# The remainder of nearly every weight tile is made by VectorE instead of GpSimd

## The reference, cut to what matters

```python
def second_block(x, ...):
    for i in range(2):
        h = rms_norm_2(x, attn_norm[i])
        proj = h @ w_in[i]                                  # differential attention, then gated linear
        mix = attention_i(proj)
        cross = memory_cross_attention(mem_q, mem, ...)
        x = x + concat([mix, cross]) @ w_out[i]
        h = rms_norm_2(x, ffn_norm[i])
        x = x + conv_ffn(h, w_up[i], conv_w[i], conv_b[i], w_down[i])

def conv_ffn(h, w_up, conv_w, conv_b, w_down):
    u = h @ w_up                                            # 1024 -> 2 * 2816
    a, g = split(causal_conv3(u, conv_w) + conv_b)
    return (silu(g) * a) @ w_down                           # 2816 -> 1024
```

## Time and profile before

| what | value |
|---|---|
| median of 3 runs | 1799.42 us (1798.91 to 1802.1) |
| profiled execution | 1797.66 us |
| its span in the trace | 1795.9 us |
| mean granted TensorE clock | 0.988 |
| TensorE busy | 1735.1 us, 97% |
| VectorE busy | 945.7 us, 53% |
| GpSimd busy | 746.8 us, 42% |

### The profile page before, as it was taken

How to read it: one execution, slowest core, us unless ns; L and a number is a source line. 1 busy time by engine, 2 the same in 40 slices (tenths; PEclk the granted TensorE clock), 3 DMA queues, 4 the chain that set the end, 5 groups by cost and what they waited for, 6 DMA issues and landing times.

```text
span 1795.9 us, 28022 instructions
## 1 busy us (share of the span) xinstructions
PE 1735.1 (97%) x11634; PEld 1403.9 (78%) x11634; DVE 945.7 (53%) x1610; ACT 477.8 (27%) x1039; POOL 746.8 (42%) x372
## 2 busy tenths in 40 slices
PE   8999989999899999899999999999999999999999
PEld 7678768887667777777888888877876788888887
DVE  6676245666655376746655551234434466665311
ACT  3111123445232354423222220123121332222100
POOL 3333135200544132237555554553233665555542
PEclk9999999999899999999999999999999999999999
DMA  5222120000234122113223322221112233323332
GB/s 194 83 82 88 44 87 3 3 3 3 89 109 139 46 97 74 59 59 106 96 94 96 103 95 94 95 91 59 59 58 71 74 94 102 97 94 95 104 95 71
DMA packets 43644, 143.95 MB, mean 80 GB/s; under 512 B 5191, under 2 KB 7128, under 8 KB 43390
## 3 DMA queue, kind: packets, MB, share of 16 engines
q1 hardware_dynamic: 43518, 142.15, 24.8%
HBM read 139.50 MB, written 4.08 MB: 80 GB/s over the span
## 4 chain that ended last, share of the span: by engine, by line
PE 66%; DVE 3%; ACT 2%; issue 1%; POOL 0%; DMA 0%; DVEq 0%; SPq 0%; ACTq 0%
PE all_p_bank L214 20%; PE all_p_bank L216 19%; PE all_p_bank L215 19%; PE all_p_bank L2553 1%; PE all_p_bank L2582 1%; PE all_p_bank L2340 1%; PE all_p_bank L2316 1%; PE all_p_bank L2570 0%; PE all_p_bank L2067 0%; PE all_p_bank L3050 0%; PE all_p_bank L3032 0%; PE all_p_bank L3045 0%; PE all_p_bank L2327 0%; POOL b_wlo L195 0%; PE all_p_bank L2516 0%
## 5 line engine op out<-in xcount | busy, mean ns | idle before, releaser
L195 POOL TENSOR_TENSOR b_wlo<-b_raw,b_whi 128x1024 fp32r<-128x1024 f32 x235 | 576.2, 2455 | 748.2 <-DVE b_whi L181 745.6
L214 PE MATMUL all_p_bank<-b_hi,b_whi 128*128 128x512 f32 x1232 | 498.7, 405 | 7.7 <-issue 6.1
L216 PE MATMUL all_p_bank<-b_hi,b_wlo 128*128 128x512 f32 x1232 | 482.8, 392 | 0.0
L215 PE MATMUL all_p_bank<-b_lo,b_whi 128*128 128x512 f32 x1232 | 482.7, 392 | 0.0
L181 DVE CAST b_whi<-b_raw 128x1024 fp32r<-128x1024 f32 x238 | 184.7, 782 | 424.1 <-PE all_p_bank L216 410.3
L214 PEld LDWEIGHTS all_p_bank<-b_hi,b_whi 128*128 128x128 f32 x1232 | 233.0, 189 | 72.4 <-issue 26.1
L216 PEld LDWEIGHTS all_p_bank<-b_hi,b_wlo 128*128 128x128 f32 x1232 | 232.9, 189 | 49.9
L215 PEld LDWEIGHTS all_p_bank<-b_lo,b_whi 128*128 128x128 f32 x1232 | 233.0, 189 | 49.5 <-issue 4.1
L214 PE MATMUL all_p_bank<-f_mhi,b_whi 128*128 128x512 f32 x352 | 136.9, 389 | 0.0
L215 PE MATMUL all_p_bank<-f_mlo,b_whi 128*128 128x512 f32 x352 | 136.9, 389 | 0.0
L216 PE MATMUL all_p_bank<-f_mhi,b_wlo 128*128 128x512 f32 x352 | 136.9, 389 | 0.0
(11 more groups left out here) (459 smaller groups left out, 2566.4 us busy)
## 6 DMA issues: line engine op xcount, KB each, us to landing
b_raw<-in_w_up SPq DMA_DIRECT2D x88, 512.0 KB, 3.5
b_raw<-in_w_down SPq DMA_DIRECT2D x44, 512.0 KB, 3.5
b_raw<-in_w_in SPq DMA_DIRECT2D x32, 512.0 KB, 3.5
b_raw<-in_w_out SPq DMA_DIRECT2D x24, 512.0 KB, 3.6
b_raw<-in_w_gla SPq DMA_DIRECT2D x22, 512.0 KB, 3.5
b_raw<-in_w_diff SPq DMA_DIRECT2D x20, 512.0 KB, 3.5
b_raw<-in_w_mem SPq DMA_DIRECT2D x8, 512.0 KB, 3.6
all_x<-in_x SPq DMA_DIRECT2D x8, 256.0 KB, 5.6
```

The source lines that it names most:

```text
L195: self.nc.gpsimd.tensor_tensor(self.lo[:, n % SLOTS, :], self.raw[:, n % RAWS, :], self.hi[:, n % SLOTS, :].bitcast(F32), ALU.subtract).th ...
L214: nc.tensor.matmul(acc, lhsT=left[0], rhs=right[0], start=first, stop=False)
L215: nc.tensor.matmul(acc, lhsT=left[0], rhs=right[1], start=False, stop=False)
L216: return nc.tensor.matmul(acc, lhsT=left[1], rhs=right[0], start=False, stop=last)
```

## The change

A list of ranges of tiles is added to the ring. For a tile in a range, VectorE makes the remainder right behind its cast, and GpSimd skips it. The one range goes from the second program's fifth tile to the last tile of all. At the border each engine waits once for the other (`s_lo`), so that the remainders are counted in order: VectorE's first remainder waits for GpSimd's last. Nothing else is written differently: the plan, the loads and TensorE's list stay.

```diff
@@ class Ring
+        self.ranges = []
@@ def round(self, dve, upto)
             self.nc.vector.tensor_copy(self.hi[:, n % SLOTS, :], self.raw[:, n % RAWS, :]).then_inc(self.s_hi, 1)
             self.rounded = n + 1
+            if self.whole(n):
+                if not self.whole(n - 1):
+                    dve.wait_ge(self.s_lo, n)
+                self.low(dve, n)
+
+    def whole(self, n):
+
+        return any(a <= n < b for a, b in self.ranges)
 
     def split(self, dve, n):
 
         self.round(dve, n)
+        self.low(dve, n)
+
+    def low(self, dve, n):
+
         dve.wait_ge(self.s_hi, n + 1)
         self.nc.vector.tensor_tensor(self.lo[:, n % SLOTS, :], self.raw[:, n % RAWS, :],
                                      self.hi[:, n % SLOTS, :].bitcast(F32), ALU.subtract).then_inc(self.s_lo, 1)
@@ def rest(self, pool, upto)
         for n in range(self.rested, min(upto + 1, len(self.tiles), self.limit)):
+            self.rested = n + 1
+            if self.whole(n):
+                continue
+            if self.whole(n - 1):
+                pool.wait_ge(self.s_lo, n)
             pool.wait_ge(self.s_hi, n + 1)
             self.nc.gpsimd.tensor_tensor(...)
-            self.rested = n + 1
@@ def upper_layers
+    c.ring.ranges = [(base + 4, len(c.ring.tiles))]
     run(nc, u.ring, base, plan + plan3, TwoLayers(low, high), Sides(*side, *side3), begin, store)
```

## The result

The changed kernel takes 1813.26 us (median of 4 runs, 1810.76 to 1814.18), the one before 1799.78 us on the same chip. The ratio is 1.0070, 95% interval 1.0057 to 1.0083. So the change costs 13.5 us by the medians and 12.6 by the ratio, where I had forecast 0.4 us less, that is no difference. The profiled execution has a span of 1812.4 us against 1795.9; it is the longest of the four and the one before the shortest of its kernel, so the 16.5 us between them are more than the change costs.

A forecast was written before the change was run, and what follows sets the result against it. TensorE, busy 97% of the span, was taken as the bound. Five places summed to -0.45 us, other waits and feed-forward blocks to nothing: 1799.42 - 0.45 = 1799.0 us, forecast's own range 1796.5 to 1801.5, 8 in 10 1794 to 1803.5.

The forecast's parts named there:

- Price of a moved remainder: Each remainder moved to VectorE adds 1.25 us to its list where nothing hides it; bounds 1.23 and 2.455.
- What is given back: VectorE operations stretched during GpSimd's subtractions fall back to short values, such as 2.82 to 0.68 us at line 2616.
- The five places: Five TensorE waits in the attention stages, 9.1 us together, that the change touches most; net sum -0.45 us.
- at 650: TensorE's wait of 1.09 us at 650.72: one cast's remainder adds 1.25, line 2656 gives back 0.39; net +0.86.
- the chain of 747 and 759: TensorE's waits of 2.99 and 3.01 us, one chain on VectorE and ScalarE from 740.10 on; net -1.4 us.
- 1238: TensorE's wait of 1.26 us at 1238.39: two casts add 0.7, line 2366 gives back 1.85; net -1.16.
- 1376: TensorE's wait of 0.76 us at 1376.69: remainder stands before a bank's emptying, nothing given back; net +1.25.
- The other waits of the attention stages: Remaining attention waits and the two norms ahead of the feed-forward blocks: taken as 0, bounded by say 2 us.
- Feed-forward blocks cost nothing: In the feed-forward blocks each pair has 3.4 us to spare, falling to 2.2, so TensorE sees nothing.
- Faster by the clock: Rival: shorter waits spare two stretches at 1.2 GHz behind 747 and 759; -3.9 us, 1795.5 us; chance 0.20.
- Nothing is given back: Rival: long VectorE rows have another cause, or the lock only changes hands; +6.8, 1806.2 us; chance 0.12.
- Taps late by 21 us: Rival: taps too late by 0.5 in each of 42 feed-forward pairs; +21 us, 1820 us; chance 0.03.

The follow-up runs named there:

- e2: Against the kernel before, VectorE makes the remainders of layer two's 40 attention tiles alone; 1802.92 us, ratio 1.0018.
- e12: Against the kernel before, VectorE makes the remainders of layer three's 30 attention tiles except four, which stay with GpSimd; 1797.98 us, ratio 0.9997.
- e5: The changed kernel's 202 remainders on VectorE, each made one to three steps later in its list; 1801.82 us, ratio 1.0021 to the kernel before.
- e1: Against the kernel before, VectorE makes the remainders of the two feed-forward blocks' 132 tiles alone; 1802.02 us, ratio 1.0010.
- e10: Against the kernel before, VectorE makes six attention tiles' remainders, one pair's only behind a side step; 1796.05 us, ratio 0.9971.

## Why the prediction was wrong, step by step

- **Price of a moved remainder, 1.25 us of the list: right**, 0.69 and 1.23 in the rows at 632. But only 163 of 205 took 1.22 or 1.23 us. The other 42 took 2.19 or 2.20, each beside a GpSimd operation:

```profile
867.63 0.69 DVE L182 CAST b_whi<-b_raw 128x1024 fp32r<-128x1024 f32 x1 [0.46 <-PE all_p_bank L233]
867.91 1.56 POOL L756 TENSOR_TENSOR f_mlo<-f_m,f_mhi 128x512 fp32r<-128x512 f32 x1 [9.32 <-ACT f_mhi L740]
868.36 2.20 DVE L201 TENSOR_TENSOR b_wlo<-b_raw,b_whi 128x1024 fp32r<-128x1024 f32 x1
```

The mean, 1424 ns, missed the 1.22 to 1.3 that I had named. These rows are what the sentence cited from the Trainium skill ("SBUF — State Buffer", "SBUF: two separate sides") says for a VectorE operation with two SBUF inputs; the trace agrees, 2.20 against 1.23 us, and on GpSimd's side 2.24 against 1.28. I had cited it and given it no term.

- **What is given back: right.** Lines 2633, 2676 and 2383 have in the changed kernel

```profile
755.07 0.68 DVE L2633 TENSOR_TENSOR l_o<-l_o,l_ss 128x512 f32<-128x512 f32 x1
...
767.45 0.75 DVE L2676 SCALAR_TENSOR_TENSOR l_sc<-l_sc,l_rs 128x512 f32<-128x512 f32 x1
...
1247.40 0.16 DVE L2383 SCALAR_TENSOR_TENSOR l3m_nbm<-l3m_mxm,l3m_rqm 128x2 f32<-128x2 f32 x1
```

against 2.82, 2.79 and 2.01. No row of the first two lines is over 0.75 any more.

- **The five places: right, one by one.** From the aligned traces, counted up to each of the five matmuls: at 650 +0.9 (forecast +0.86), of which +1.1 comes as a new wait for line 2658, 1.6 us ahead of the wait that I named, and that one shrank by 0.2; the chain of 747 and 759 -1.4 (-1.4); 1238 -1.2 (-1.16); 1376 +1.3 (+1.25). Together -0.4, forecast -0.45. In the chain, 747 shrank by 1.7 as worked out. The two remainders of the second pair are paid as the wait of 2.62 for line 2658, and the wait at 759 shrank by about what line 2659 gives back.

- **The step that failed: "The other waits of the attention stages … I take them as 0, bounded by one moved remainder and one stretched operation each way, say 2 us".** The attention stages gave +13.7 us, so about 14 lie outside the five places. The bound had no ground: I looked at waits that the trace before shows, and the change made waits where there were none, or lengthened others. They are places where a cast stood in front of an operation that frees a bank or feeds TensorE with less to spare than the remainders take: 2.4 us at 636.80 for two of them, 0.46 each at two more places in layer two, 0.66 for `l3q_sq` and 0.9 more at 1289 in layer three, and 1.05 for `l_mlo` at 1424. In att 2a there is one of 1.17 at 511.96, which is 0.56 in e2's trace. These waits are about half of the 14 us. The other half is a second term that the sum put at nothing: TensorE at 1.2 GHz behind them, 1.6 us behind 636.80 and 4.8 in layer three, where the prediction had one such stretch, behind 1376, as something that "adds a little". That one came too, 1.6 us. All this is read from one trace each. e12 puts a number on how few the places are: without 4 of 30 tiles layer three's loss is gone. e5 shows, for layer two, that it is place and not amount.

- **Feed-forward blocks cost nothing: right in the traces** (+0.3 and +0.1 us; 134 matmuls in 30 us at full clock, VectorE at 26.29 of 30 us instead of 17.73, where the sum had 24.5, because the stretched remainders are mostly here):

```profile
900.00:930.00 30.00, 30.00 (x134) 24.85 (x133) 26.29 (x31) 7.36 (x11) 4.66 (x3) 1.00 0.28 89
```

With e1's 0.1% (interval 0.01 to 0.20%) I can't exclude 1 or 2 us.

- **The rivals.** None of them covers 1813 us with what happened. "Faster by the clock" was right in one place. Behind 747 the shorter wait did spare the stretch at 1.2 GHz (granted clock 1.00, where the earlier trace rows have 0.72):

```profile
757.00:759.00 2.00, 2.00 (x19) 1.78 (x17) 1.90 (x5) 0.63 (x2) 0.00 (x0) 1.00 0.21 82
```

But the 1.4 us won went into the next wait, for `l_mlo` at 761.68, which grew from 1.10 to 2.58: just what the prediction had held against this rival. Behind 759 the stretch stayed. Over the whole program the sign was the other way, and the mean granted clock fell from 0.988 to 0.983. "Nothing is given back" was wrong in its own words, yet the part "the lock only changes hands" happened to one remainder in five. Taps late by 21 us did not happen.

## What to carry to other kernels

When work goes from an idle engine into a busy engine's list, don't ask only which existing waits it touches. Take every place where it would stand, name the next operation behind it that frees a bank or feeds the limiting engine, and read how much that operation had to spare; where it is less than the added time, put the work behind it. And if two engines disturb each other, move only the few operations whose disturbance lies on the path: 4 tiles gained 0.3%, all 202 cost 0.7%, and 42 at places behind the next side step gained 0.6%.

## What the runs showed of the hardware that I had not expected

- In the changed kernel the blocking between VectorE and GpSimd went both ways, against the one that began second. 42 remainders on VectorE that began during a GpSimd operation took 2.19 or 2.20 us instead of 1.23; three GpSimd operations that began during a remainder, `l_mlo` among them, took 2.24 to 2.35, where `l_mlo` takes 1.28 alone.
- A wait of 2.36 us was followed by 4 us at a mean granted clock of 0.59, the same place without the wait had 1.00. This wait cost 1.7 times its length. Behind a new wait of only 0.66 us (1229.65) the clock was 0.58 for 4 us as well.
- In parts of the program that no kernel changes, single executions differ by up to 6 us at the same matmul (start column), and a gain of 2.8 us seen in one trace (e10) was not there in the times. When such a stretch at the lower clock falls elsewhere, or is missing, stays open.
